# Delta stage of a two-block network: gate softplus in token layout, cumulative sums by a triangular matrix of ones

## The chip, the cores and the metric

The kernel runs on one NeuronCore of a Trainium2 chip. The metric is the device time of one execution in microseconds (us). Its engines are named as the profile names them: PE (TensorE, the matrix products; PEld is its load of the stationary operand), DVE (VectorE), ACT (ScalarE), POOL (GpSimd) and SP (SyncE, which only issues DMAs here). A tensor lies in on-chip memory over 128 partitions; an operation on "16x256" uses 16 partitions and 256 elements in each.

## The reference

The input is one sequence of 256 tokens with 1024 features. Ten stages follow each other, each adding to the residual: twice (hybrid attention, gated FFN with a short convolution), then FFN, short convolution mixer, FFN, FFN, gated DeltaNet mixer ("Delta stage"), FFN. Only the Delta stage is touched. Its projection gives, beside 32 tiles of keys, queries and values, two gates for each of 16 value heads and each token:

```
beta = sigmoid(b)
g    = -exp(a_log) * softplus(a + dt_bias)      # a, b: [token, head]
```

Within each chunk of 128 tokens the stage needs the cumulative sum G of g over the tokens: as a column (token on the partition, one number per head) and as a row broadcast to all partitions (token along the free dimension). exp(G_i - G_j) is the decay between two tokens of a chunk, exp(G_i) the decay of the carried state. The keys' triangular system is solved per head and chunk, and the rest are products.

## The kernel before, in words

All engines run one program in order and are tied by semaphores. The Delta stage's first panel of weights gives the gates (bank 7 of PSUM: b in partitions 0 to 15, a in partitions 32 to 47, tokens along the free dimension). Then slots t = 0 to 46 follow. In slot t (t < 32) PE multiplies tile t of the projection (24 products, L2108 to L2110; every fp32 factor is split into a high and a low part), DVE scales it out of PSUM (delta_read, L1824; PE's tile t waits for the read of tile t-2), ACT starts the convolution (delta_tap, L1164), DVE does its other three taps one slot later (delta_taps, L1831), and ACT applies SiLU and squares (delta_silu, L1184 and L1189). Each slot also splits one panel of weights: ACT makes the high part (L943) and DVE the low part (L1409). Heads go in four sets of four, n = 0 to 3, eight tiles each; delta_step(s, n, o) is what set n does in slot t = 8n + o: rows of G (delta_rows, L2498), masked exponents (delta_exponent, L1898), decays (delta_decay, L1221 and L1229), sums of squared keys (L2508) and key products (delta_kk, L2533), the matrix of the triangular system (delta_amat, L1944). The matrix goes through a relay in HBM (SP: L776, L778) to DVE's solver (L1972, L1973) and back.

Around the change the order is written out by hand in the slot loops of each engine. In slot 1 DVE does the softplus on 16x256 tiles and scans each chunk (delta_gates_softplus, L1855 to L1878). In slot 3 PE transposes the results (delta_turn_gates, L2462), DVE copies them (delta_gates_turned, L1880), ACT takes exp(G) (L1213), and DVE negates it after waiting for ACT (L1889). In slot 4 (ROWS_AT) PE makes the rows of set 0, each by a product of a broadcast unit column with the 16 rows of G. PE's program has the key sums and key products of set 0 right after the transposes in slot 3, and tile 4 behind those. ACT loads a table (ACT_TABLE_LOAD) when the function changes between the groups Exp, Ln, SiLU and Sqrt.

Of the kernel before, what the change touches and what calls it, by code (L numbers as in the profile page):

```python
# [91 lines left out]
def column_map(stages):  # L92

    at, n = {}, 0

    def add(key, count):
        nonlocal n
        at[key] = n
        n += count
    for s, (kind, i) in enumerate(stages):  # L100
        add(("pre", s), KT)
        if kind == HYBRID:
            add(("qk_gain", s), 8)
            add(("cmp_gain", s), 1)
            add(("gate_b", s), 2)
            add(("gla_gain", s), 1)
        if kind == FFN1:
            add(("tap", s), 3 * FT)
            add(("conv_b", s), FT)
        if kind == SHORT:  # L110
            add(("tap", s), 3 * KT)
        if kind == DELTA:
            add(("tap", s), WIDTH * 4 * KH)
            add(("out_norm", s), 1)
            add(("a_log", s), 1)
            add(("dt_bias", s), 1)
    return at, n
# [70 lines left out]
def lay_out(stages, w):  # L188
# [14 lines left out]
    for kind, i in stages:  # L203
# [56 lines left out]
        if kind == DELTA:  # L260
# [15 lines left out]
            late = np.zeros((P, 2), w_in.dtype)  # L276
            late[ROW_A:ROW_A + VH, 0] = w["gdn_a_log_2"][0]
            late[ROW_A:ROW_A + VH, 1] = w["gdn_dt_bias_2"][0]
            cols += [conv_cols, columns(w["gdn_norm_w_2"][0]), late]
# [14 lines left out]
def build(nc, stages, arrays):  # L294
# [14 lines left out]
    with ExitStack() as ctx:  # L309
# [83 lines left out]
        g_cum = carve("g_cum", [ROW_A + VH, S])  # L393
# [4 lines left out]
        a_rate = carve("a_rate", [ROW_A + VH, 1])  # L398
# [534 lines left out]
        def _(act):  # L933
# [267 lines left out]
            def delta_gates(s):  # L1201
# [5 lines left out]
                act.activation(a_rate[a, :], col(("a_log", s))[a, :], ACT.Exp).then_inc(d["gate_act"], 1)  # L1207
# [7 lines left out]
            def delta_decay(s, n):  # L1215
# [8 lines left out]
                act.wait_ge(d["gate_tok"], 3)  # L1224
# [135 lines left out]
            def delta(s):  # L1360
                hi_to(first_panel[s] + 3)
                delta_gates(s)
                for t in range(SLOTS_D):
# [7 lines left out]
                    if t == 3:  # L1371
                        delta_gates_turned(s)
# [22 lines left out]
        def _(dve):  # L1395
# [459 lines left out]
            def delta_gates_softplus(s):  # L1855
                a, b = slice(ROW_A, ROW_A + VH), slice(0, VH)

                dve.wait_ge(d["gate_act"], 1)
                link(dve.tensor_scalar(gates[b, 1, :], gates[b, 1, :], 1.0, None, ALU.add))
                dve.reciprocal(gates[b, 0, :], gates[b, 1, :]).then_inc(d["gates_ready"], 1)  # L1860

                dve.wait_ge(d["gate_act"], 4)
                e, m, ln = gates[a, 2, :], gates[a, 1, :], gates[a, 3, :]
# [7 lines left out]
                link(dve.scalar_tensor_tensor(out=m, in0=gates[a, 0, :], scalar=0.0, in1=ln,  # L1871
                                              op0=ALU.max, op1=ALU.add))
                link(dve.tensor_scalar(e, m, a_rate[a, :], -1.0, ALU.mult, ALU.mult))
# [6 lines left out]
            def delta_gates_turned(s):  # L1880

                dve.wait_ge(d["gate_turned"], 1)
                by_chunk = lambda b, o: bank[b][:, o:o + CHUNKS * VH].rearrange("p (c h) -> p c h", c=CHUNKS)
                dve.tensor_copy(g_tok[:], by_chunk(7, 256)).then_inc(d["gate_tok"], 1)
                dve.tensor_copy(beta_tok[:], by_chunk(6, 0)).then_inc(d["gate_tok"], 1)
                dve.wait_ge(d["gate_tok"], 2)
                dve.tensor_scalar(neg_g[:], g_tok[:], -1.0, None, ALU.mult).then_inc(d["gate_tok"], 1)
                dve.wait_ge(d["tok_exp"], 1)
                link(dve.tensor_scalar(neg_eg[:], neg_eg[:], -1.0, None, ALU.mult))  # L1889
# [215 lines left out]
        def _(pe):  # L2105
# [356 lines left out]
            def delta_turn_gates(s):  # L2462
                pe.wait_ge(d["gates_ready"], 3)
                for c in range(CHUNKS):
                    cs = slice(c * P, (c + 1) * P)
                    o = 256 + VH * c

                    pe.transpose(bank[6][:, VH * c:VH * (c + 1)], gates[0:VH, 0, cs], ident[0:VH, 0:VH])
                    last = pe.transpose(bank[7][:, o:o + VH], g_cum[ROW_A:ROW_A + VH, cs],
                                        ident[ROW_A:ROW_A + VH, ROW_A:ROW_A + VH])  # L2470
                last.then_inc(d["gate_turned"], 1)
# [15 lines left out]
            def delta_rows(s, n):  # L2487
# [243 lines left out]
            def delta(s):  # L2731
                delta_gates(s)
                for t in range(SLOTS_D):
# [37 lines left out]
```

## Time and profile before

| | us |
|---|---|
| median of 3 runs | 2166.47 |
| lowest, highest | 2163.2, 2168.67 |
| the profiled execution | 2163.57 |
| its span in the trace | 2161.8 |
| PE busy in it | 2066.7 (96%) |
| DVE busy | 1447.0 (67%) |
| ACT busy | 1111.4 (51%) |

The span is what the trace covers from the first to the last record; the execution's own time is 1.8 us more. PE's busy share counts a product from its start to its modelled end. The mean granted clock of PE is 0.982 of full speed (2.4 GHz); where it is 0.50 the clock is 1.2 GHz. The Delta stage starts at about 1612 us and ends at about 1885 us of the span.

### The profile page before, as it was taken

The numbers are of one execution on the slowest core, as the hardware profiler recorded it, in microseconds if no ns is written. First come the engines' busy times: TensorE is split into PE (matmuls) and PEld (weight loads), VectorE is DVE, ScalarE is ACT, GpSimd is POOL, SyncE is SP. The second block draws the span as 40 slices with busy tenths as digits, with TensorE's granted clock in tenths as the row PEclk, the third lists the DMA queues.
The fourth block names the chain that finished last, engine by engine and source line by source line (L and its number), as shares of the span: only waits on it lengthen the run. The fifth ranks groups of instructions, "written<-read, shape, count | busy, mean of one in ns | idle before, by whom it ended". The sixth has DMA issues, their size and how long they took to land.

```text
span 2161.8 us, 41596 instructions
## 1 busy us (share of the span) xinstructions
PE 2066.7 (96%) x15668; PEld 1928.9 (89%) x15668; DVE 1447.0 (67%) x2490; ACT 1111.4 (51%) x1802; POOL 49.6 (2%) x63
## 2 busy tenths in 40 slices
PE   7998999999999999999999999999997898999998
PEld 7897889989988899999999999999986898989997
DVE  4567777774677777775567765575668886467555
ACT  4564455554654555554454544454456665546443
POOL 1001000000020000000000000000000000000000
PEclk9999999999999999999999999999998998999999
DMA  8533465553423555555556455555543433335552
GB/s 252 170 118 108 148 208 191 186 171 120 137 98 117 178 192 187 191 179 193 183 159 212 153 194 194 170 187 183 185 168 108 145 112 99 118 132 175 191 184 97
DMA packets 118585, 350.93 MB, mean 162 GB/s; under 512 B 23504, under 2 KB 36120, under 8 KB 117952
## 3 DMA queue, kind: packets, MB, share of 16 engines
q1 hardware_dynamic: 115248, 336.27, 47.2%
q0 software_dynamic: 3216, 12.97, 2.2%
q8 instruction: 85, 1.39, 0.3%
q14 instruction: 36, 0.29, 0.0%
HBM read 341.85 MB, written 7.34 MB: 162 GB/s over the span
## 4 chain that ended last, share of the span: by engine, by line
PE 76%; DVE 12%; ACT 6%; issue 3%; DMA 3%; POOL 0%; SPq 0%; DVEq 0%; ACTq 0%; POOLq 0%
PE bank L2108 23%; PE bank L2110 22%; PE bank L2109 22%; DVE wlo L1409 4%; ACT whi L943 3%; PE bank L2567 2%; DMA raw<-panels 1%; PE bank L2276 1%; DVE arena L1448 1%; DMA relay<-arena 1%; DVE arena L1972 1%; DVE arena L1973 1%; DVE arena L1612 1%; DMA arena<-relay 0%; PE bank L2142 0%
## 5 line engine op out<-in xcount | busy, mean ns | idle before, releaser
L2108 PE MATMUL bank<-xhi,whi 128*128 128x256 f32 x3496 | 1004.4, 287 | 24.6 <-DVE arena L1612 10.1
L2109 PE MATMUL bank<-xlo,whi 128*128 128x256 f32 x3496 | 989.5, 283 | 0.0
L2110 PE MATMUL bank<-xhi,wlo 128*128 128x256 f32 x3496 | 989.0, 283 | 0.0
L1409 DVE TENSOR_TENSOR wlo<-raw,whi 128x1024 fp32r<-128x1024 f32 x623 | 742.4, 1232 | 204.9 <-ACT whi L943 203.9
L2108 PEld LDWEIGHTS bank<-xhi,whi 128*128 128x128 f32 x3496 | 666.2, 191 | 46.3 <-DVE arena L1612 12.5
L2109 PEld LDWEIGHTS bank<-xlo,whi 128*128 128x128 f32 x3496 | 666.2, 191 | 5.4
L2110 PEld LDWEIGHTS bank<-xhi,wlo 128*128 128x128 f32 x3496 | 665.7, 190 | 0.0
L943 ACT ACTIVATE whi<-raw 128x1024 fp32r<-128x1024 f32 x623 | 623.5, 1046 | 49.4 <-DVE arena L1609 19.0
L2108 PE MATMUL bank<-whi,hhi 128*128 128x512 f32 x688 | 274.4, 399 | 2.7 <-DVE hlo L1561 1.2
L2110 PE MATMUL bank<-whi,hlo 128*128 128x512 f32 x688 | 272.8, 397 | 0.0
L2109 PE MATMUL bank<-wlo,hhi 128*128 128x512 f32 x688 | 272.5, 396 | 0.0
L1014 ACT ACTIVATE hhi<-h 128x256 fp32r<-128x256 f32 x172 | 71.9, 418 | 273.6 <-PE bank L2110 151.2
L1561 DVE TENSOR_TENSOR hlo<-h,hhi 128x256 fp32r<-128x256 f32 x156 | 66.4, 426 | 182.3 <-ACT hhi L1014 182.3
L996 ACT ACTIVATE act_out<-first 128x256 f32<-128x256 f32 x92 | 38.4, 418 | 242.0 <-DVE first L1539 235.5
L2110 PEld LDWEIGHTS bank<-whi,hlo 128*128 128x128 f32 x688 | 129.9, 189 | 30.8
L2108 PEld LDWEIGHTS bank<-whi,hhi 128*128 128x128 f32 x688 | 129.9, 189 | 27.9 <-issue 4.6
L2109 PEld LDWEIGHTS bank<-wlo,hhi 128*128 128x128 f32 x688 | 130.4, 190 | 24.6
L1539 DVE TENSOR_TENSOR first<-bank,rstd 128x256 f32<-128x256 f32 x132 | 55.8, 423 | 57.7 <-PE bank L2110 57.4
L1559 DVE TENSOR_TENSOR h<-act_out,second 128x256 f32<-128x256 f32 x136 | 57.9, 426 | 42.1 <-ACT act_out L1005 21.6
L1001 ACT ACTIVATE conv<-first,cols 128x256 f32<-128x256 f32 x44 | 26.5, 602 | 93.1 <-DVE first L1539 93.1
L1061 ACT ACTIVATE arena<-arena 128x256 f32<-128x256 f32 x48 | 20.0, 417 | 102.1 <-DVE arena L1612 102.1
L1540 DVE TENSOR_TENSOR second<-bank,rstd 128x256 f32<-128x256 f32 x132 | 54.9, 416 | 0.0
(361 smaller groups left out, 1708.5 us busy)
## 6 DMA issues: line engine op xcount, KB each, us to landing
raw<-panels SPq DMA_DIRECT2D x623, 512.0 KB, 4.3
arena<-w_in POOLq DMA_DIRECT2D x2, 2048.0 KB, 10.7
arena<-relay SPq DMA_DIRECT2D x8, 512.0 KB, 4.2
arena<-gains_in POOLq DMA_DIRECT2D x6, 512.0 KB, 4.1
relay<-arena POOLq DMA_DIRECT2D x4, 512.0 KB, 7.8
relay<-arena SPq DMA_DIRECT2D x4, 512.0 KB, 5.0
bias_table<-arena POOLq DMA_DIRECT2D x1, 1536.0 KB, 35.1
x<-x_in SPq DMA_DIRECT2D x1, 1024.0 KB, 4.8
```

The costliest lines, as they stand in the source:

```text
L943: act.activation(whi[slot][:], raw[slot][:], ACT.Copy).then_inc(hi_done, 1)
L996: act.activation(act_out[:, sl, :], first[:, sl, 2:], ACT.Silu).then_inc(act_done, 1)
L1014: act.activation(hhi[:, sl, :], h[:, sl, :], ACT.Copy).then_inc(hhi_done, 1)
L1409: dve.tensor_tensor(wlo[slot][:], raw[slot][:], whi[slot][:].bitcast(F32), ALU.subtract) \
L1539: dve.tensor_tensor(first[:, sl, 2:], pair[:, 0:S], rstd[:], ALU.mult).then_inc(gate_scaled, 1)
L1540: dve.tensor_tensor(second[:, sl, :], pair[:, S:], rstd[:], ALU.mult).then_inc(pair_read, 1)
L1559: dve.tensor_tensor(h[:, sl, :], gated, second[:, sl, :], ALU.mult).then_inc(h_done, 1)
L1561: dve.tensor_tensor(hlo[:, sl, :], h[:, sl, :], hhi[:, sl, :].bitcast(F32), ALU.subtract) \
L2108: pe.matmul(dst, w_hi, a_hi, start=start, stop=False, skip_group_check=True)
L2109: pe.matmul(dst, w_hi, a_lo, start=False, stop=False, skip_group_check=True)
L2110: return pe.matmul(dst, w_lo, a_hi, start=False, stop=stop, skip_group_check=True)
L2567: last = pe.matmul(dst[:, m * P:(m + 1) * P], lhs(m), rhs(m), start=True, stop=True)
```

## The change

- The softplus moves from 16x256 tiles (16 partitions, 256 tokens each) to a layout with the token on the partition: 128x32 (two chunks by 16 heads).
- For that, PE turns the raw gates (the exponentials of b and a, the logarithm, and a itself: eight transposes) in slot 2, and DVE's softplus stands in slot 2 instead of slot 1, with the copy out of PSUM and a comparison that makes `until`, the 128x128 matrix of ones on and above the diagonal.
- The two scans go. Slot 3 has instead two products of `until` with the per-token gates.
- The rows of G are made by products of a broadcast gate column (128 partitions) with `until`, one for each head and chunk: eight products of 128 columns for each set of heads, where there were four of 256.
- exp(G) on ACT moves from slot 3 to slot 4 (ROWS_AT), and its negation on DVE to slot 6. The factor exp(a_log) is taken on 128x16, for which the constants get 15 more columns.

```diff
@@ ScalarE, gates
-                act.activation(a_rate[a, :], col(("a_log", s))[a, :], ACT.Exp).then_inc(d["gate_act"], 1)
+                at = col_at[("a_log", s)]
+                act.activation(a_rate, cols[:, at:at + VH], ACT.Exp).then_inc(d["gate_act"], 1)
@@ ScalarE, slot loop
-                    if t == 3:
+                    if t == ROWS_AT:
                         delta_gates_turned(s)
@@ VectorE
             def delta_gates_softplus(s):
-                a, b = slice(ROW_A, ROW_A + VH), slice(0, VH)
-
-                dve.wait_ge(d["gate_act"], 1)
-                link(dve.tensor_scalar(gates[b, 1, :], gates[b, 1, :], 1.0, None, ALU.add))
-                dve.reciprocal(gates[b, 0, :], gates[b, 1, :]).then_inc(d["gates_ready"], 1)
-
+
+                dve.tensor_scalar(until, masks[:, 2, :], -1.0, None, ALU.is_ge).then_inc(d["gates_ready"], 1)
+                dve.wait_ge(d["gate_turned"], 1)
                 dve.wait_ge(d["gate_act"], 4)
-                e, m, ln = gates[a, 2, :], gates[a, 1, :], gates[a, 3, :]
+                m, pre, e, ln = (gates_turned[:, v, :, :] for v in range(4))
+                by = lambda v: v.rearrange("p (c h) -> p c h", c=CHUNKS)
+                link(dve.tensor_copy(gates_turned[:, 1:, :, :].rearrange("p v c h -> p (v c h)"),
+                                     bank[7][:, CHUNKS * VH:4 * CHUNKS * VH]))
+                link(dve.tensor_scalar(m, by(bank[6][:, 0:CHUNKS * VH]), 1.0, None, ALU.add))
+                link(dve.reciprocal(beta_tok[:], m))
...
-                for c in range(CHUNKS):
-                    cs = slice(c * P, (c + 1) * P)
-                    dve.tensor_tensor_scan(g_cum[a, cs], ones[a, :], gates[a, 2, cs], 0.0, ALU.mult, ALU.add) \
-                        .then_inc(d["gates_ready"], 1)
...
+            def delta_gates_summed(s):
+
+                dve.wait_ge(d["gate_turned"], 2)
+                sums = bank[7][:, 256:256 + CHUNKS * VH].rearrange("p (c h) -> p c h", c=CHUNKS)
+                dve.tensor_copy(g_tok[:], sums).then_inc(d["gate_tok"], 1)
+                dve.tensor_scalar(neg_g[:], sums, -1.0, None, ALU.mult).then_inc(d["gate_tok"], 1)
+
+            def delta_gates_negated(s):
+
                 dve.wait_ge(d["tok_exp"], 1)
                 link(dve.tensor_scalar(neg_eg[:], neg_eg[:], -1.0, None, ALU.mult))
@@ VectorE, slot loop
-                    if t == 1:
+                    if t == 2:
                         delta_gates_softplus(s)
                     if t == 3:
-                        delta_gates_turned(s)
+                        delta_gates_summed(s)
+                    if t == ROWS_AT + 2:
+                        delta_gates_negated(s)
@@ TensorE
             def delta_turn_gates(s):
-                pe.wait_ge(d["gates_ready"], 3)
+                pe.wait_ge(d["gate_act"], 4)
+                pe.wait_ge(d["gates_scaled"], 2)
+                pe.wait_ge(rstd_ready, s + 1)
+                for v, (row, i) in enumerate(((0, 1), (ROW_A, 0), (ROW_A, 2), (ROW_A, 3))):
+                    rows = slice(row, row + VH)
+                    for c in range(CHUNKS):
+                        o = (CHUNKS * v + c) * VH
+                        last = pe.transpose(bank[7 if v else 6][:, o:o + VH], gates[rows, i, c * P:(c + 1) * P], ident[rows, rows])
+                last.then_inc(d["gate_turned"], 1)
+
+            def delta_sum_gates(s):
+                pe.wait_ge(d["gates_ready"], 2)
                 for c in range(CHUNKS):
...
+                    last = pe.matmul(bank[7][:, o:o + VH], until, a_tok[:, c, :], start=True, stop=True)
                 last.then_inc(d["gate_turned"], 1)
@@ TensorE, delta_rows
-                        r = ROW_A + SET * n + 2 * g + hh
-                        last = pe.matmul(bank[6 + g][:, hh * S:(hh + 1) * S],
-                                         ident[ROW_A:ROW_A + VH, r:r + 1].to_broadcast([VH, P]),
-                                         g_cum[ROW_A:ROW_A + VH, :], start=True, stop=True)
+                        head = SET * n + 2 * g + hh
+                        for c in range(CHUNKS):
+                            o = hh * S + c * P
+                            last = pe.matmul(bank[6 + g][:, o:o + P], a_tok[:, c, head:head + 1].to_broadcast([P, P]),
+                                             until, start=True, stop=True)
@@ TensorE, slot loop
+                    if t == 2:
+                        delta_turn_gates(s)
                     if t == 3:
-                        delta_turn_gates(s)
+                        delta_sum_gates(s)
```

The order of instructions on three engines follows. Line numbers of the changed kernel are 2 to 13 higher: the read L1824 is L1827 there, the taps L1831 are L1834, the low split L1409 is L1412, on ACT L943 is L945, L1184 is L1186, on PE L2508 is L2521 and L2533 is L2546.

DVE before, slots 1 and 2: the second read and the taps of tile 0, then the gates, then the third read.

```order
L1824 TENSOR_TENSOR arena<-bank5,rstd 128x256
L1831 SCALAR_TENSOR_TENSOR conv<-arena,cols,conv 128x256 x3
L1859 TENSOR_SCALAR arena<-arena 16x256
L1860 RECIPROCAL arena<-arena 16x256
L1864 TENSOR_SCALAR arena<-arena 16x256
L1865 TENSOR_TENSOR arena<-arena 16x256
L1866 SCALAR_TENSOR_TENSOR arena<-arena 16x256
...
L1877 SCALAR_TENSOR_TENSOR arena<-ones,arena 16x128 x2
L1409 TENSOR_TENSOR wlo5<-raw5,whi5 128x1024
L1824 TENSOR_TENSOR arena<-bank4,rstd 128x256
```

DVE now, the same slots.

```order
L1827 TENSOR_TENSOR arena<-bank5,rstd 128x256
L1834 SCALAR_TENSOR_TENSOR conv<-arena,cols,conv 128x256 x3
L1412 TENSOR_TENSOR wlo5<-raw5,whi5 128x1024
L1827 TENSOR_TENSOR arena<-bank4,rstd 128x256
L1834 SCALAR_TENSOR_TENSOR conv<-arena,cols,conv 128x256 x3
L1860 TENSOR_SCALAR arena<-masks 128x128
L1865 COPY arena<-bank7 128x96
L1867 TENSOR_SCALAR arena<-bank6 128x32
L1868 RECIPROCAL arena<-arena 128x32
L1870 TENSOR_SCALAR arena<-arena 128x32
...
L1878 SCALAR_TENSOR_TENSOR arena<-arena 128x32
```

The split of a panel, the read of tile 2 and the taps of tile 1 now stand ahead of the gates. Eleven operations on 16 partitions have become twelve on 128.

PE before, slot 3, behind tile 3: transposes, key sums, key products.

```order
L2468 MATMUL bank6<-masks,arena 128x16
L2469 MATMUL bank7<-masks,arena 128x16
L2468 MATMUL bank6<-masks,arena 128x16
L2469 MATMUL bank7<-masks,arena 128x16
L2508 MATMUL bank3<-ones,sq 128x1 x4
L2533 MATMUL bank2<-arena 128x128 x4
```

PE now: the eight transposes behind tile 2, and behind tile 3 the two sums ahead of key sums and products.

```order
L2115 MATMUL bank4<-xhi,wlo3 128x256
L2475 MATMUL bank6<-masks,arena 128x16 x2
L2475 MATMUL bank7<-masks,arena 128x16 x6
L2113 MATMUL bank5<-xhi,whi4 128x256
...
L2482 MATMUL bank7<-arena 128x16 x2
L2521 MATMUL bank3<-ones,sq 128x1 x4
L2546 MATMUL bank2<-arena 128x128 x4
```

What tile 4 waits behind in PE's order is the same but for the sums; the transposes stand one tile earlier.

ACT before, end of slot 3 and slot 4, from the SiLU of tile 2 to the exponentials of set 0.

```order
L1184 ACTIVATE arena<-conv 128x256
L1189 ACTIVATE sq<-arena 128x256
L1213 ACT_TABLE_LOAD
L1213 ACTIVATE arena<-arena 128x32
L1164 ACTIVATE conv<-arena,cols 128x256
L943 ACTIVATE whi2<-raw2 128x1024
L1184 ACT_TABLE_LOAD
L1184 ACTIVATE arena<-conv 128x256
L1189 ACTIVATE sq<-arena 128x256
L1221 ACT_TABLE_LOAD
L1221 ACTIVATE arena<-bank6 128x256
```

ACT now.

```order
L1186 ACTIVATE arena<-conv 128x256
L1191 ACTIVATE sq<-arena 128x256
L1166 ACTIVATE conv<-arena,cols 128x256
L945 ACTIVATE whi2<-raw2 128x1024
L1186 ACTIVATE arena<-conv 128x256
L1191 ACTIVATE sq<-arena 128x256
L1216 ACT_TABLE_LOAD
L1216 ACTIVATE arena<-arena 128x32
L1224 ACTIVATE arena<-bank6 128x256
```

Two of three table loads are gone, and the small exponential of G stands directly ahead of those of the rows.

## Rows read from the trace of the kernel before

**Rows 1.** The page: span, and the chain that ended last by engine.

```profile
span 2161.8 us, 41596 instructions
...
PE 76%; DVE 12%; ACT 6%; issue 3%; DMA 3%; POOL 0%; SPq 0%; DVEq 0%; ACTq 0%; POOLq 0%
```

**Rows 2.** Busy time by window: length, engines' busy us (instructions), clock, DMA share, GB/s.

```profile
1612.00:1640.90 28.90, 19.83 (x128) 18.98 (x126) 20.55 (x40) 15.35 (x24) 3.24 (x4) 0.76 0.50 167
```

**Rows 3.** Timeline of DVE, slot 1: start, duration, engine, line, [idle before].

```profile
1621.63 1.52 DVE L1831 SCALAR_TENSOR_TENSOR conv<-arena,cols,conv 128x256 f32<-128x256 f32 x3
1623.06 0.28 DVE L1859 TENSOR_SCALAR arena<-arena 16x256 f32<-16x256 f32 x1
1623.37 1.74 DVE L1860 RECIPROCAL arena<-arena 16x256 f32<-16x256 f32 x1
...
1628.54 0.73 DVE L1877 TENSOR_TENSOR_SCAN arena<-ones,arena 16x128 f32<-16x128 f32 x2
```

**Rows 4.** Timeline of PE, slots 3 and 4.

```profile
1621.77 0.39 PE L2108 MATMUL bank<-xhi,whi 128*128 128x256 f32 x1 [2.23 <-DVE arena L1824]
...
1626.13 0.28 PE L2110 MATMUL bank<-xhi,wlo 128*128 128x256 f32 x1
1629.32 0.29 PE L2468 MATMUL bank<-masks,arena 16*128 16x16 f32 x1 [2.92 <-DVE arena L1877]
...
1633.24 1.87 PE L2508 MATMUL bank<-ones,sq 128*128 128x1 f32 x8 [3.53 <-ACT sq L1189]
1634.97 2.05 PE L2533 MATMUL bank<-arena 128*128 128x128 f32 x8
1636.68 0.56 PE L2108 MATMUL bank<-xhi,whi 128*128 128x256 f32 x1
...
1640.84 1.99 PE L2498 MATMUL bank<-arena,masks 16*128 16x256 f32 x8
```

**Rows 5.** Timeline of ACT, slots 1 to 4.

```profile
1624.97 0.42 ACT L1189 ACTIVATE sq<-arena 128x256 f32<-128x256 f32 x1
...
1632.78 0.42 ACT L1189 ACTIVATE sq<-arena 128x256 f32<-128x256 f32 x1
...
1642.88 1.28 ACT L1184 ACT_TABLE_LOAD   x1
...
1645.06 1.28 ACT L1221 ACT_TABLE_LOAD   x1
```

**Rows 6.** Timeline of DVE, slots 4 and 5.

```profile
1640.95 0.42 DVE L1824 TENSOR_TENSOR arena<-bank,rstd 128x256 f32<-128x256 f32 x1 [1.66 <-PE bank L2110]
...
1648.28 2.30 DVE L1944 SCALAR_TENSOR_TENSOR arena<-bank,arena 128x128 f32<-128x128 f32 x8 [0.52 <-ACT arena L1229]
...
1651.16 1.22 DVE L1409 TENSOR_TENSOR wlo<-raw,whi 128x1024 fp32r<-128x1024 f32 x1
```

**Rows 7.** Groups by shape, DVE, whole span: count, busy us, mean ns, idle before.

```profile
L1795 DVE TENSOR_SCALAR second<-second,row_inv 128x128 f32<-128x128 f32 x12 | 3.4, 287 | 0.4
...
L1655 DVE RECIPROCAL qk_inv<-qk_ms 128x32 f32<-128x32 f32 x2 | 0.7, 354 | 0.1
...
L1884 DVE COPY arena<-bank 128x32 f32<-128x32 f32 x1 | 0.2, 183 | 0.0
L1887 DVE TENSOR_SCALAR arena<-arena 128x32 f32<-128x32 f32 x1 | 0.2, 181 | 0.0
```

**Rows 8.** The chain in order of time, two pieces on PE (start, us, what).

```profile
1724.07 1.92 PE bank L2498 x8
...
1729.88 1.78 PE bank L2567 x16
```

**Rows 9.** Busy time by window where PE's clock was lowered, columns as in Rows 2.

```profile
1629.00:1639.20 10.20, 6.35 (x32) 6.24 (x33) 7.81 (x16) 6.05 (x10) 0.00 (x0) 0.50 0.30 103
...
1888.50:1898.60 10.10, 8.73 (x28) 7.45 (x29) 3.01 (x9) 2.41 (x5) 0.00 (x0) 0.50 0.00 1
```

**Rows 10.** One line's instructions on PE: duration of one, min/median/max ns.

```profile
L2567 PE MATMUL bank<-arena x256: 272/275/580, 1678.6 to 1879.6; 128*128 128x128 f32 x128
```

More of the change, by code:

```diff
@@ L114, in column_map @@
             add(("out_norm", s), 1)
-            add(("a_log", s), 1)
+            add(("a_log", s), VH)
             add(("dt_bias", s), 1)
@@ L275, in lay_out @@
             conv_cols = w["gdn_conv_w_2"][0].reshape(WIDTH, 4 * KH, P)[:, order].reshape(-1, P).T
[L276 to L279, printed above, removed]
+            rates = np.repeat(w["gdn_a_log_2"][0][None, :], P, 0)
+            late = np.zeros((P, 1), w_in.dtype)
+            late[ROW_A:ROW_A + VH, 0] = w["gdn_dt_bias_2"][0]
+            cols += [conv_cols, columns(w["gdn_norm_w_2"][0]), rates, late]
         if kind == FFN1:
@@ L392, in build @@
         o_all = carve("o_all", [P, 2 * SET, S])
-        g_cum = carve("g_cum", [ROW_A + VH, S])
+        until = carve("until", [P, P])
+        gates_turned = carve("gates_turned", [P, 4, CHUNKS, VH])
+        a_tok = carve("a_tok", [P, CHUNKS, VH])
         blk_a = carve("blk_a", [P, BLK * BLK])
@@ L397, in build @@
         blk_tmp = carve("blk_tmp", [P, BLK * BLK // 4])
-        a_rate = carve("a_rate", [ROW_A + VH, 1])
+        a_rate = carve("a_rate", [P, VH])
         g_tok = carve("g_tok", [P, CHUNKS, VH])
@@ L1223, in delta_decay @@
                                    ACT.Exp).then_inc(d["eg"], 1)
-                act.wait_ge(d["gate_tok"], 3)
+                act.wait_ge(d["gate_tok"], 2)
                 for g in range(KSET):
@@ L1869, in delta_gates_softplus @@
                 link(dve.tensor_tensor(ln, ln, m, ALU.add))
-                link(dve.scalar_tensor_tensor(out=m, in0=gates[a, 0, :], scalar=0.0, in1=ln,
-                                              op0=ALU.max, op1=ALU.add))
-                link(dve.tensor_scalar(e, m, a_rate[a, :], -1.0, ALU.mult, ALU.mult))
-                for c in range(CHUNKS):
-                    cs = slice(c * P, (c + 1) * P)
-                    dve.tensor_tensor_scan(g_cum[a, cs], ones[a, :], gates[a, 2, cs], 0.0, ALU.mult, ALU.add) \
-                        .then_inc(d["gates_ready"], 1)
[L1880 to L1887, printed above, removed]
+                link(dve.scalar_tensor_tensor(out=m, in0=pre, scalar=0.0, in1=ln, op0=ALU.max, op1=ALU.add))
+                dve.scalar_tensor_tensor(out=a_tok, in0=m, scalar=-1.0,
+                                         in1=a_rate.rearrange("p (o h) -> p o h", o=1).to_broadcast([P, CHUNKS, VH]),
+                                         op0=ALU.mult, op1=ALU.mult).then_inc(d["gates_ready"], 1)
+            def delta_gates_summed(s):
[4 more added lines that the diff above has]
+            def delta_gates_negated(s):
                 dve.wait_ge(d["tok_exp"], 1)
@@ L2462, in delta_turn_gates @@
             def delta_turn_gates(s):
-                pe.wait_ge(d["gates_ready"], 3)
+                pe.wait_ge(d["gate_act"], 4)
[9 more added lines that the diff above has]
+                pe.wait_ge(d["gates_ready"], 2)
                 for c in range(CHUNKS):
-                    cs = slice(c * P, (c + 1) * P)
                     o = 256 + VH * c
-                    pe.transpose(bank[6][:, VH * c:VH * (c + 1)], gates[0:VH, 0, cs], ident[0:VH, 0:VH])
-                    last = pe.transpose(bank[7][:, o:o + VH], g_cum[ROW_A:ROW_A + VH, cs],
-                                        ident[ROW_A:ROW_A + VH, ROW_A:ROW_A + VH])
+                    last = pe.matmul(bank[7][:, o:o + VH], until, a_tok[:, c, :], start=True, stop=True)
                 last.then_inc(d["gate_turned"], 1)
```

## The prediction

> **What bounds the kernel now.** I read the chain of waits first. 76% of the span is PE [rows 1], and the reader should see that almost everywhere the kernel is a row of products that nothing outside PE shortens. So a change in VectorE work pays only where PE waits. Next I read busy time by window: in the 28.90 us from the start of the Delta stage to the end of its tile 4, PE is busy 19.83 us, at a mean clock of 0.76 [rows 2]. The head of this stage is a place where PE waits, for 9 us.
>
> The timelines say for what. Tile 3 starts at 1621.77, when DVE has read tile 1, and its last product, which starts at 1626.13, ends at 1626.41; then PE waits 2.92 us for DVE's scan, transposes at 1629.32, and waits 3.53 us for ACT's square of the second key tile (1632.78 + 0.42 = 1633.20) [rows 4, 5]. That square is late because DVE does the taps of tile 1 behind the gates: the gates hold DVE from 1623.06 to 1628.54 + 0.73 = 1629.27, 6.2 us, of which the reciprocal on 16x256 is 1.74 [rows 3]. Behind the square come key sums and key products (1633.24 to 1636.68, 3.44 us) and tile 4 (1636.68 to 1640.84, 4.16 us) [rows 4]. DVE, which has nothing left, reads tile 4 at 1640.95 after 1.66 us of idleness [rows 6]. From there set 0 goes through ACT's exponentials, DVE's matrix (L1944), the relay and the solver; everything later in the kernel hangs on this chain.
>
> **The change part by part.**
>
> *VectorE, slots 1 and 2.* The taps of tile 0 end at about 1623.1 [rows 3]. Now the split of a panel, the read of tile 2 and the taps of tile 1 follow at once: 1.22 + 0.42 + 1.52 [rows 3, 6] = 3.2, so they end at 1626.3. The gates follow: `until`, one 128x128 operation, 0.29 [rows 7]; a copy of 128x96 out of PSUM, between 0.18 (128x32) and 0.29 (128x128), taken as 0.25 [rows 7]; the addition, 0.18; the reciprocal of 128x32, 0.35, where the one of 16x256 took 1.74 [rows 3, 7]; eight operations of 128x32 at 0.18 = 1.44 [rows 7]. Sum 2.5, and with gaps of 0.03 behind each of twelve linked operations (as from 1623.06 + 0.28 to 1623.37 [rows 3]) 2.9. They end at 1629.2, practically when they end now. The bounds for this block are 2.5 (no gaps) and 3.5 (every small operation as long as the 128x128 one: 12 x 0.29). So the gates are not earlier; what is earlier is the square of tile 1. Its ACT work (tap, split, SiLU, square) took from the end of the third read to 1633.20. Counted from the square of tile 0, which ends at 1625.39 [rows 5], it needs the same four operations: I put its end at 1627.8, an estimate, with 1.5 us to spare. This wait, which ends last now, is then covered.
>
> *TensorE, slots 2 and 3.* The eight transposes fall into the 2.23 us that PE waits ahead of tile 3 [rows 4]. Four of the kind are seen to start within about 0.15 us and take 0.29 each, so eight need less than a microsecond: hidden, and they cost their length only if that cover were gone. What they wait for (the gates of ACT) is done before tile 2 ends, since ACT's program has them ahead of the tap of tile 0. The two sums wait for the gates at 1629.2 and take some 0.3 (bounds 0.1 and 0.6, from the same 0.29 records). Then key sums and products start at 1629.4 rather than 1633.24: 3.8 us earlier. Late next is the gates' last operation, no longer a square. Queued behind the sums are the key sums, the key products and tile 4, so all of them move: tile 4 runs from 1632.9 and ends at 1637.0 rather than 1640.84. I keep the durations, 3.44 and 4.16, because the clock was 0.50 over the whole of 1629.0 to 1639.2 [rows 9], and PE has again been mostly idle ahead.
>
> *VectorE and ScalarE, slots 3 and 4.* DVE's two small operations of slot 3 replace four, and its wait for ACT's exp(G) goes to slot 6; DVE idles before tile 4 anyway, so 0. On ACT the table load of 1.28 ahead of tile 3's SiLU goes [rows 5], because SiLU stays loaded; the load ahead of the exponentials stays, and behind it comes the small exponential (about 0.2). This makes the decays 1.0 us earlier after tile 4. DVE waits for them only 0.52 us before L1944 [rows 6]; its own work (taps of tile 4) ends there, so 0.5 is what comes through, and the split at 1651.16, behind which SP sends the relay, is earlier by that. Bounds: 0.2 and 1.0. Only one set has this order, once.
>
> *Rows of G.* Per set, eight products of 128 columns on 128 rows, so 16 records, for four products of 256 columns on 16 rows, 8 records in 1.92 us on the chain. The nearest row is 16 records of fp32 128x128 with 128 columns in 1.78 us [rows 8]. So -0.14 a set if they overlap alike; if they did not overlap at all, 16 x 0.275 = 4.4, +2.5 a set [rows 10]. Each has a broadcast column as the stationary operand, as the products of the unit column have now, so I take the overlapped price, 0 for four sets, and keep -0.6 and +9.9 as ends.
>
> Here the Trainium skill speaks against the change: "TensorE: Matmul & The Clock Gate", section "LDWEIGHTS (loading the stationary operand)", says that a load costs its columns, 128/1.2 = 107 ns, however few rows it has, so narrow stationary operands were no dearer, and the change doubles the loads. Paid in full, 8 more loads in 4 sets would be an estimated 3.4 us, and the sum would be a gain of 0.9 instead of 4.3. But 16 records in 1.78 us [rows 8] already hold a load each, so the trace does not charge them.
>
> *The rest.* The 15 more columns of constants are loaded at the start with the others: 0.
>
> **Sum.** 3.8 + 0.5 = 4.3 us earlier at the relay of set 0. After that no engine has anything that did not move with it: SP's loads are released by DVE's splits, the solver by the relay, and the last stage is products. So the shift should arrive at the end. Against the profiled execution that is 2163.57 - 4.3 = 2159.3. That one lies 2.9 below the median of the three runs; against the median it is 2166.47 - 4.3 = 2162.2, my forecast. The spread of the three runs is 5.5 us, as large as the gain. What can move it is the clock: stretches at 0.50 of 10.20 and 10.10 us with PE busy 6.35 and 8.73 [rows 9] cost half of that busy time, 3.2 and 4.4 us. A shift of the chain by 4 us can lengthen or shorten such a stretch: +-3 us, an estimate.
>
> **The rivals.**
>
> *The clock comes back earlier.* With less idleness in the head, PE may be at 2.4 GHz for key products and tile 4. Against it: it still idles about 3 us after tile 3. For it: one wait where there were two, and transposes in a third. Key sums and products at half their price are 1.7 rather than 3.44, tile 4, half of whose 4.16 us was slow, loses about 1.2: 2.9 more in all, 2159.3. Shorter slow stretches later could take it to 2156.5.
>
> *The gain is lost on the way.* A slow stretch grows at the end of the stage, where PE is nearly full, or the square of tile 1 is not ready after all, because the panel that ACT splits ahead of it lands late. Half of one such stretch, 3 us, or the 3.8 of the square, leaves 2166. The DMA share of 0.50 in the head [rows 2] makes a late panel unlikely.
>
> *Slower: the row products do not overlap.* One mechanism, on PE ahead of tile 5 of every set, where L2498 stands on the chain at 1.92 [rows 8]. It decides from 3.0 us a set (4.3/4 = 1.08 more), that is 0.19 us a record. At 0.275 a record [rows 10] it costs +9.9, total +5.6: 2172.1; if each is also preceded by its own load it is beyond 2173. For it: stationary and moving operands are now full 128 rows and there are twice as many. Against it: all other fp32 products of this shape overlap to 0.11 us.
>
> **How the numbers follow.** Forecast, 2162.2, own range 2159 to 2166: 0.55. Clock earlier, 2159.3: 0.22. Gain lost, 2166: 0.17. Rows not overlapped, 2172.1: 0.06. This kernel can be told from no change at about 0.3%, 6.5 us: faster means below 2160.0, slower above 2173.0. Faster gets most of the clock's case and a little of the forecast's, 0.19 + 0.07 = 0.26; slower 0.04; the rest, 0.70, is within 0.3%. The range, 2156.5 to 2168.5, holds the first three cases and leaves about 0.1 on either side.
>
> **What would show it.** In the changed profile PE's wait ahead of the key sums is gone and the one ahead of the sums of gates is about 2.8 us, ended by DVE's last gate operation; twelve gate operations in 2.5 to 3.5 us; the read of tile 4 at 1637 (the stage starting alike); one table load of ACT between it and the exponentials; L1944 6.8 us after that read instead of 7.3; rows of G at 1.8 to 2.0 us per set. Wrong would be: a wait on a square ahead of the key sums, row products above 3 us, or a solver of set 0 that starts at 1661 as now.

## The result and the profile after

| | before | changed |
|---|---|---|
| median on the same chip, us | 2164.84 (4 runs) | 2152.44 (4 runs, 2151.41 to 2153.32) |
| ratio to before, 95% interval | 1 | 0.994 [0.9923, 0.9958] |
| profiled execution | 2163.57 | 2152.31 |
| its span | 2161.8 | 2150.5 |
| PE busy | 2066.7 | 2054.4 |

The changed kernel is 12.4 us faster by the medians and 11.3 by the spans. Forecast were 4.3. The forecast, 2162.2, and the whole range down to 2156.5 lie above the result. The 0.6% is beyond the 0.3% that can be told from no change.

The head of the Delta stage comes first, since it is where the prediction looked. DVE of the changed kernel, slots 0 to 5 of the stage (answers to [rows 3, 6]):

```profile
1615.63 0.42 DVE L1827 TENSOR_TENSOR arena<-bank,rstd 128x256 f32<-128x256 f32 x1
...
1619.05 1.52 DVE L1834 SCALAR_TENSOR_TENSOR conv<-arena,cols,conv 128x256 f32<-128x256 f32 x3
1620.48 0.22 DVE L1860 TENSOR_SCALAR arena<-masks 128x128 f32<-128x128 f32 x1
...
1621.13 0.35 DVE L1868 RECIPROCAL arena<-arena 128x32 f32<-128x32 f32 x1
...
1623.09 0.19 DVE L1878 SCALAR_TENSOR_TENSOR arena<-arena 128x32 f32<-128x32 f32 x1
...
1631.70 0.42 DVE L1827 TENSOR_TENSOR arena<-bank,rstd 128x256 f32<-128x256 f32 x1 [4.19 <-PE bank L2115]
...
1638.39 2.15 DVE L1947 SCALAR_TENSOR_TENSOR arena<-bank,arena 128x128 f32<-128x128 f32 x8
...
1650.87 0.17 DVE L1975 TENSOR_TENSOR arena<-arena 64x15 f32<-64x15 f32 x1 [0.62 <-DMA arena<-relay]
```

PE of the changed kernel, slots 2 to 4 (answers to [rows 4]):

```profile
1613.62 0.55 PE L2475 MATMUL bank<-masks,arena 16*128 16x16 f32 x8
...
1616.10 0.56 PE L2113 MATMUL bank<-xhi,whi 128*128 128x256 f32 x1 [1.94 <-DVE arena L1827]
...
1623.34 1.03 PE L2482 MATMUL bank<-arena 128*128 128x16 f32 x4 [2.61 <-DVE arena L1878]
1624.21 1.85 PE L2521 MATMUL bank<-ones,sq 128*128 128x1 f32 x8
1625.92 2.05 PE L2546 MATMUL bank<-arena 128*128 128x128 f32 x8
1627.62 0.56 PE L2113 MATMUL bank<-xhi,whi 128*128 128x256 f32 x1
...
1631.50 1.95 PE L2512 MATMUL bank<-arena 128*128 128x128 f32 x16
```

The reader should see one wait of 2.61 us ahead of the sums of gates (L2482), ended by DVE's last gate operation, and no wait on a square ahead of the key sums (L2521) where [rows 4] have 3.53. The transposes (0.55) run ahead of a wait of PE that is there anyway. ACT of the changed kernel has one table load between the last square and the exponentials (answers to [rows 5]):

```profile
1621.40 0.42 ACT L1191 ACTIVATE sq<-arena 128x256 f32<-128x256 f32 x1
...
1633.59 0.42 ACT L1186 ACTIVATE arena<-conv 128x256 f32<-128x256 f32 x1
1634.04 0.42 ACT L1191 ACTIVATE sq<-arena 128x256 f32<-128x256 f32 x1
1634.48 1.28 ACT L1216 ACT_TABLE_LOAD   x1
1635.77 0.23 ACT L1216 ACTIVATE arena<-arena 128x32 f32<-128x32 f32 x1
```

From DVE's read of tile 1 (1621.29 before, 1615.63 after) to its read of tile 4 (1640.95 [rows 6]; 1631.70) the kernel before takes 19.66 us and the changed one 16.07: 3.6 less. That is close to the forecast. But the read of tile 1 itself comes 5.7 us earlier, and in both kernels the gates stand behind that read; of what the diff changes only the eight transposes of PE (0.55 us) and ACT's exponential of a_log, now on 128x16, can stand ahead of it. The gain began long before this stage. At the other end, the last stage, an FFN that the diff does not touch, is shorter too. The same two DVE operations, one early in that stage and the kernel's last, first before:

```profile
1914.29 0.43 DVE L1559 TENSOR_TENSOR h<-arena,second 128x256 f32<-128x256 f32 x1
...
2154.76 2.74 DVE L1463 SCALAR_TENSOR_TENSOR x<-arena,post_rstd,x 128x512 f32<-128x512 f32 x4
```

and in the changed kernel:

```profile
1905.03 0.43 DVE L1562 TENSOR_TENSOR h<-arena,second 128x256 f32<-128x256 f32 x1
...
2143.48 2.74 DVE L1466 SCALAR_TENSOR_TENSOR x<-arena,post_rstd,x 128x512 f32<-128x512 f32 x4
```

The lead is 5.7 us at the read of tile 1, 10.3 at the first operation of the solver (1661.14 before, 1650.87 after), 9.3 early in the last stage and 11.3 at the end. So 5.7 + 2.0 us come from stages without a changed instruction, and 3.6 from between. Where in the earlier stages the lead arises shows DVE's split of the same two panels, first before:

```profile
935.63 1.23 DVE L1409 TENSOR_TENSOR wlo<-raw,whi 128x1024 fp32r<-128x1024 f32 x1 [0.78 <-ACT whi L943]
...
1596.87 1.23 DVE L1409 TENSOR_TENSOR wlo<-raw,whi 128x1024 fp32r<-128x1024 f32 x1 [0.52 <-ACT whi L943]
```

and in the changed kernel:

```profile
936.20 1.23 DVE L1412 TENSOR_TENSOR wlo<-raw,whi 128x1024 fp32r<-128x1024 f32 x1 [0.78 <-ACT whi L945]
...
1591.04 1.23 DVE L1412 TENSOR_TENSOR wlo<-raw,whi 128x1024 fp32r<-128x1024 f32 x1 [0.52 <-ACT whi L945]
```

At 936 us the changed kernel is still 0.6 us behind. Between these two splits (called the long section below) it takes 654.8 us and the kernel before 661.2: 6.4 us less, the whole lead. The section is one of almost pure products. Busy time by window in the kernel before, columns as in Rows 2:

```profile
860.00:1240.00 380.00, 378.21 (x2716) 355.12 (x2715) 262.68 (x397) 192.21 (x282) 1.06 (x2) 1.00 0.54 180
1240.00:1600.00 360.00, 359.14 (x2531) 335.65 (x2531) 222.27 (x316) 167.60 (x238) 0.53 (x1) 1.00 0.56 184
```

and in the changed kernel:

```profile
860.00:1240.00 380.00, 377.12 (x2729) 353.91 (x2728) 264.54 (x401) 193.37 (x284) 1.06 (x2) 1.00 0.54 182
1240.00:1600.00 360.00, 358.70 (x2559) 335.76 (x2559) 225.56 (x324) 171.73 (x248) 0.53 (x1) 1.00 0.56 185
```

PE is full in both and its granted clock 1.00 in both, yet in the same 740 us it does 5288 products instead of 5247. These 41, at 740/5247 = 0.141 us each, are 5.8 us. A product itself is quicker. Timeline of PE, a product and the 21st behind it, before:

```profile
1010.48 0.28 PE L2108 MATMUL bank<-xhi,whi 128*128 128x256 f32 x1
...
1012.97 0.28 PE L2108 MATMUL bank<-xhi,whi 128*128 128x256 f32 x1
```

and in the changed kernel:

```profile
1010.31 0.28 PE L2113 MATMUL bank<-xhi,whi 128*128 128x256 f32 x1
...
1012.77 0.28 PE L2113 MATMUL bank<-xhi,whi 128*128 128x256 f32 x1
```

That is 2.49/21 = 118.6 ns from start to start against 2.46/21 = 117.1. Over all products of 256 columns between 800 and 1000 us that start within 130 ns of the one before, the mean is 118.4 and 116.8 ns (called the pace below). The kernel has 3 x 3496 = 10488 such products, so 1.6 ns each would be 16.8 us if PE always ran at that pace; where it waits or its clock is lowered, the pace is not collected.

### The profile page after: what moved, and what is told of

Same layout as the page of the kernel before. It is cut to its first block and busy times, and to the rows that moved or that the text cites. A ratio compares the mean times of both kernels' runs of the same rounds, so it can differ in the third digit from the quotient of the medians.

```text
span 2150.5 us, 41675 instructions
## 1 busy us (share of the span) xinstructions
PE 2054.4 (96%) x15708; PEld 1920.4 (89%) x15708; DVE 1441.9 (67%) x2489; ACT 1108.5 (52%) x1800; POOL 49.6 (2%) x63
## 3 DMA queue, kind: packets, MB, share of 16 engines
HBM read 341.86 MB, written 7.34 MB: 162 GB/s over the span
## 5 line engine op out<-in xcount | busy, mean ns | idle before, releaser
L1412 DVE TENSOR_TENSOR wlo<-raw,whi 128x1024 fp32r<-128x1024 f32 x623 | 742.1, 1231 | 202.4 <-ACT whi L945 201.1
L945 ACT ACTIVATE whi<-raw 128x1024 fp32r<-128x1024 f32 x623 | 623.5, 1046 | 50.7 <-DVE arena L1612 20.7
```

The costliest lines, as they stand in the source:

```text
L945: act.activation(whi[slot][:], raw[slot][:], ACT.Copy).then_inc(hi_done, 1)
L1412: dve.tensor_tensor(wlo[slot][:], raw[slot][:], whi[slot][:].bitcast(F32), ALU.subtract) \
```

## The experiments

What the diff changes for those stages is one thing: the constants `cols` grow from 435 to 450 columns. With its padding this tensor takes 1824 instead of 1760 bytes of each partition, and everything declared behind it (`ones`, `x`, the moving operands `xhi`, `xlo`, `hhi`, `hlo`, the arena) lies 64 bytes further. The split weights `whi` and `wlo`, declared ahead of it, stay. **Theory A**: the address of the moving operand relative to the weights sets the pace, and the new table only happens to move it. **Rival B**: the edit of the Delta stage does it, or something in its code that also works elsewhere. **Rival C**: the tensors behind `xhi` and `xlo`, in which most other engines work, are what matters.

Placements below are bytes in a partition. `xhi` starts at 96 modulo 128 before and at 32 after; the weights at 0 in both. The three groups of runs are from three chips, each with its own runs of before: medians 2163.89 (e1 to e4), 2165.96 (e5 to e8) and 2164.64 (e9 to e12). Ratios with their intervals are to these runs; they are not quotients of the medians and differ from them by up to 0.0009. A difference between runs of two groups carries the difference of the chips with it, up to 2 us.

### e1: only the shift

```diff
         cols = sb("cols", [P, n_cols])
+        gap = sb("gap", [P, 16])
```

> The kernel before, with an unused tensor of 64 B per partition behind the constants, so that every later tensor of on-chip memory starts where it starts in the changed kernel. No instruction differs. Theory A (the 5.9 us gained before the Delta stage and 2.0 us in the last stage come from the addresses): about 8 us faster, 2157, products of 256 columns 116.8 ns apart instead of 118.4. Rival B (they come from where the constants lie in HBM, from the code or from the runs): no change, 2165.

Measured: 2156.98, ratio 0.9973 [0.9962, 0.9985], pace 116.9 ns. The kernel before, with 64 unused bytes in it, is 6.9 us faster, and its long section takes 654.9 us, as in the changed kernel. Window of e1:

```profile
1240.00:1600.00 360.00, 358.69 (x2558) 335.52 (x2556) 226.22 (x325) 171.87 (x250) 0.53 (x1) 1.00 0.55 184
```

2558 products, as the changed kernel's 2559, where before has 2531. No instruction of the Delta stage differs here, so rival B cannot explain this.

### e2: the change with the old addresses

```diff
         cols = sb("cols", [P, n_cols])          # in the changed kernel
+        gap = sb("gap", [P, 112])
```

This puts `xhi` at 96 modulo 128 again, and at the same place modulo 512 as before.

> The changed kernel with 448 B unused behind the constants: later tensors lie 512 B above their place in the kernel before, so at the same place in every 512 B. Theory A: about 8 us slower than the changed kernel, 2160.5, and products 118.4 ns apart again; then the rest, about 4 us against before, is the edit of the Delta stage, as forecast (4.3). Rival B: stays at 2152.4.

Measured: 2161.56, 0.9991 [0.9982, 1.0001], pace 118.35. Window of e2:

```profile
1240.00:1600.00 360.00, 359.15 (x2531) 335.57 (x2530) 222.54 (x316) 167.25 (x236) 0.53 (x1) 1.00 0.55 184
```

The long section takes 661.2 us again. At the old placement the change gives 2.3 us against before, with an interval of the ratio that holds 1. At the new placement it gives 2156.98 - 2152.44 = 4.5 against e1, or 5.5 when each is taken from its own chip's before (12.4 and 6.9). By the whole time the edit of the Delta stage is thus worth a few microseconds, not told more exactly; 4.3 was the forecast.

### e3 and e4: other shifts of the kernel before

`gap` of 8 columns (e3, 32 bytes, `xhi` at 0 modulo 128) and of 24 (e4, 96 bytes, `xhi` at 64).

> The kernel before with 32 B unused: the moving operands xhi and xlo then start at a multiple of 128 B. Theory A: another time than before (2165) and than e1, product spacing different; if what counts is a start at a multiple of 64 or 128 B, it is the fastest, 2155 or below. Rival B: 2165.

> The kernel before with 96 B unused: xhi at 64 in 128 B, hhi at 32 in 64 B. If theory A holds with a multiple of 64 B, like e3; if what counts is the hhi tensors, at 64 B multiples in both given kernels, slower than before. Rival B: 2165.

Measured: e3 2177.23, 1.0061 [1.0039, 1.0083], pace 119.7. e4 2163.8, 0.9994 [0.9984, 1.0004], pace 117.8. The timeline of e3, again 21 products apart:

```profile
1010.25 0.28 PE L2109 MATMUL bank<-xhi,whi 128*128 128x256 f32 x1
...
1012.77 0.28 PE L2109 MATMUL bank<-xhi,whi 128*128 128x256 f32 x1
```

2.52/21 = 120.0 ns. So 32 unused bytes cost 13 us and 64 gain 7: the same program spreads over 20 us by its addresses alone. The pace does not order all times: e4 has a better pace than before and the same time. Its products of 512 columns (moving operand `whi` or `wlo`, stationary `hhi` or `hlo`) are slower: 234.3 ns apart against 233.0.

The long section shows both kinds at once, without the scatter of whole executions. In every kernel it has 3702 products of 256 columns and 872 of 512 (means taken within the section):

| | `xhi` modulo 128 | long section, us | 256 columns, ns | 512 columns, ns |
|---|---|---|---|---|
| before, e2, e11 | 96 | 661.2 | 118.4 | 233.0 |
| e8 | 96 | 660.3 | 118.3 | 232.0 |
| e12 | 48 | 661.3 | 118.3 | 233.3 |
| e4 | 64 | 660.1 | 117.8 | 234.3 |
| e3 | 0 | 666.8 | 119.7 | 233.9 |
| e10 | 32 | 658.7 | 118.6 | 228.2 |
| changed, e1, e5, e6, e9 | 32 | 654.8 to 654.9 | 116.8 | 231.6 to 231.7 |
| e7 | 32 | 654.9 | 116.7 | 232.7 |

The two paces account for the lengths: e4 has 3702 x 0.6 = 2.2 us less and 872 x 1.3 = 1.1 more, -1.1 where -1.2 is measured; e3 has +5.7 for +5.6, e10 -3.2 for -2.5, the changed kernel -6.9 for -6.4.

### e5: only the order of VectorE

```diff
-                    if t == 1:                  # in e1
+                    if t == 2:
                         delta_gates_softplus(s)
```

The gates keep 16x256 tiles and scans but stand behind the taps of tile 1; the 64 bytes of e1 are in.

> The kernel before at the changed kernel's addresses (e1, 2157.0) with one edit: the softplus in its old layout stands in slot 2 instead of slot 1. Theory A (the new layout makes the gain of the Delta stage, the order alone only moves the wait): the square of the second key tile is early, but the gates end 6.2 us behind the taps of tile 1, at about 1632.5 on the clock of the trace before, so the key sums start 0.4 us earlier than before: 2156.6. Rival B (the order makes the gain): 3 us or more below e1, 2154 or less.

Measured: 2156.07, 0.9963 [0.9951, 0.9974]; the interval overlaps that of e1. DVE's second read and its read of tile 4 in e5:

```profile
1614.88 0.42 DVE L1825 TENSOR_TENSOR arena<-bank,rstd 128x256 f32<-128x256 f32 x1
...
1634.33 0.42 DVE L1825 TENSOR_TENSOR arena<-bank,rstd 128x256 f32<-128x256 f32 x1 [1.45 <-PE bank L2111]
```

19.45 us where before has 19.66 and the change 16.07. The same stretch in e1, e3, e4, e7, e8 and e11, whose head is that of before, takes 19.3 to 20.4, and in e2, e6, e9, e10 and e12, whose head is the changed one, 15.9 to 16.9. So the layout's gain is clear of the scatter and the order alone gives nothing that is. PE of e5:

```profile
1625.99 0.29 PE L2469 MATMUL bank<-masks,arena 16*128 16x16 f32 x1 [6.02 <-DVE arena L1878]
...
1626.32 1.86 PE L2509 MATMUL bank<-ones,sq 128*128 128x1 f32 x8
```

The wait on the square is gone and the one on the gates has grown from 2.92 to 6.02, about the 2.92 + 3.53 of [rows 4]. The head is paid either way; only gates that are shorter *and* behind the taps shorten it. The layout is what makes them fit: 6.2 us of gates become 2.8.

### e6: exp(G) and its negation in slot 3

```diff
-                    if t == ROWS_AT:            # ScalarE, in the changed kernel
+                    if t == 3:
                         delta_gates_turned(s)
-                    if t == ROWS_AT + 2:        # VectorE
+                    if t == 3:
                         delta_gates_negated(s)
```

> The changed kernel (2152.4) with exp(G) on ACT and its negation on DVE both back in slot 3. ACT loads tables once more in slots 3 and 4 and DVE waits in slot 3. Theory A (this part is worth the 0.5 to 1.0 us seen between the read of tile 4 and the start of the solver): 2153.0 to 2153.5. Rival B (it is hidden behind tile 4): 2152.4, and L1947 starts 6.7 us after the read of tile 4 as in the changed kernel.

Measured: 2155.28, 0.9958 [0.9942, 0.9975]: 2.8 above the changed kernel's 2152.44, or 1.7 when each is taken from its own chip's before; the intervals of the two ratios overlap. DVE of e6:

```profile
1627.86 0.18 DVE L1892 TENSOR_SCALAR arena<-arena 128x32 f32<-128x32 f32 x1 [2.28 <-ACT arena L1216]
...
1630.89 0.42 DVE L1827 TENSOR_TENSOR arena<-bank,rstd 128x256 f32<-128x256 f32 x1 [1.59 <-PE bank L2115]
...
1638.22 2.30 DVE L1947 SCALAR_TENSOR_TENSOR arena<-bank,arena 128x128 f32<-128x128 f32 x8 [0.56 <-ACT arena L1232]
```

L1947 starts 7.33 us after the read of tile 4 instead of 6.69: this part is worth 0.64, nearly all of it the 0.56 that DVE waits again. It is 7.33 or 7.34 in all nine traces with exp(G) in slot 3, and 6.69 in the changed kernel, e2, e10 and e12. The wait of 2.28 in slot 3 costs nothing: 1.59 of idleness is left behind it, and the read of tile 4 comes 16.07 us behind that of tile 1 as in the changed kernel. The other 2 us of the profiled execution appear after 1680 us, away from the edit, and I did not find their cause.

### e7 and e8: which tensor's address

```diff
+        gap_a = sb("gap_a", [P, 16])            # e7 only
         xhi = sb("xhi", [P, KT, S], F32R)
         xlo = sb("xlo", [P, KT, S], F32R)
+        gap_b = sb("gap_b", [P, 112])           # e7; 16 columns in e8
```

e7 moves `xhi` and `xlo` by 64 bytes and what follows by 512; e8 moves only what follows, by 64.

> The kernel before with 64 B unused ahead of xhi and 448 B behind xlo: only xhi and xlo lie 64 B further in every 512 B, all later tensors keep their place in it. Theory A1 (the place of the moving operand xhi, xlo against the weights decides): products of 256 columns 116.9 ns apart, 6 to 7 us faster than before, 2157 to 2158. Rival A2 (the later tensors, hhi and hlo or the arena, decide): 118.4 ns, 2164.

> The kernel before with 64 B unused behind xlo: xhi and xlo stay, hhi, hlo, the arena and the rest move by 64 B. Theory A1: spacing of the 256-column products 118.4 ns, 2162 to 2164 (the 512-column products with hhi and hlo as stationary operand may win 1 ns each, 2 us). Rival A2: 2157.

Measured: e7 2154.89, 0.9957 [0.994, 0.9974], pace 116.7; e8 2167.3, 1.0003 [0.9992, 1.0014], pace 118.3. Timeline of e7:

```profile
1015.28 0.28 PE L2110 MATMUL bank<-xhi,whi 128*128 128x256 f32 x1
...
1017.73 0.28 PE L2110 MATMUL bank<-xhi,whi 128*128 128x256 f32 x1
```

and of e8:

```profile
1015.31 0.28 PE L2109 MATMUL bank<-xhi,whi 128*128 128x256 f32 x1
...
1017.79 0.28 PE L2109 MATMUL bank<-xhi,whi 128*128 128x256 f32 x1
```

2.45 against 2.48 us for 21 products. Moving the two moving operands brings the whole effect on the products of 256 columns, moving what follows none. What e8 moves does change those of 512 (233.0 to 232.0 ns), 0.9 us of the long section, too little to show in the whole time. Rival C falls for the 256 columns. The 4 us between e7 (11.1 below its chip's before) and e1 (6.9) are not the pace, since their long sections are equal; the intervals of the ratios overlap.

### e9: the rows of G twice

```diff
                             o = hh * S + c * P
-                            last = pe.matmul(bank[6 + g][:, o:o + P], a_tok[:, c, head:head + 1].to_broadcast([P, P]),
-                                             until, start=True, stop=True)
+                            for again in range(2):
+                                last = pe.matmul(bank[6 + g][:, o:o + P],
+                                                 a_tok[:, c, head:head + 1].to_broadcast([P, P]),
+                                                 until, start=True, stop=True)
```

> The changed kernel with each row product of every set made twice (the second overwrites the first with the same numbers). Theory (row products overlap and stand on the path of each set): 1.7 to 1.9 us more in each of four sets, 7 us, 2159.5. Rival (rows of sets 1 to 3 are covered by other work): 2 us or less. If the products did not overlap: 4 us a set, 2168.

Measured: 2159.77, 0.9977 [0.9967, 0.9988], 7.3 above the changed kernel. PE of e9, ahead of tile 5:

```profile
1632.38 3.73 PE L2513 MATMUL bank<-arena 128*128 128x128 f32 x32
```

32 records in 3.73 us, against 16 in 1.95: 1.8 us a set, four sets, 7.1. So the rows stand on the path in full, and their price is the overlapped one that the forecast took.

### e10: 128 bytes further

```diff
         cols = sb("cols", [P, n_cols])          # in the changed kernel
+        gap = sb("gap", [P, 32])
```

`xhi` keeps its place modulo 128 and moves from 416 to 32 modulo 512, with the weights at 128.

> The changed kernel with 128 B unused behind the constants. If the place counts within 128 B, the spacing of the 256-column products stays at 116.8 ns and the time at 2152.4; if it counts within 512 B, both change.

Measured: 2156.04, 0.9962 [0.9951, 0.9973], 3.6 above the changed kernel; pace 118.7, but the products of 512 columns go from 231.7 to 228.2 ns. Timeline of e10, 2.50 us for 21 products:

```profile
1010.04 0.28 PE L2114 MATMUL bank<-xhi,whi 128*128 128x256 f32 x1
...
1012.54 0.28 PE L2114 MATMUL bank<-xhi,whi 128*128 128x256 f32 x1
```

The place modulo 128 alone does not decide: the pattern repeats over more than 128 bytes, and it is another for the two kinds of product.

### e11: the weights moved as well

```diff
+        gap = sb("gap", [P, 16])                # in the kernel before
         whi = [sb(f"whi{i}", [P, KT * P], F32R) for i in range(RING)]
```

`xhi` lies where the changed kernel has it, but as far from the weights as before.

> The kernel before with 64 B unused ahead of the split weights: whi, wlo and all behind them lie 64 B further, so xhi lies where it lies in the changed kernel (e1, 2157.0, and e7, 2154.9), but its distance from the weights is that of the kernel before. If the place of xhi itself decides: 116.9 ns, 2157. If the distance between moving and stationary operand decides: 118.4 ns, 2164.

Measured: 2168.03, 1.0014 [1.0002, 1.0026], pace 118.4. It is 3.4 above before, but not by the pace: the profiled execution falls behind that of before in its first 250 us, and its long section takes 661.2 us as before. Timeline of e11:

```profile
1015.45 0.28 PE L2109 MATMUL bank<-xhi,whi 128*128 128x256 f32 x1
...
1017.93 0.28 PE L2109 MATMUL bank<-xhi,whi 128*128 128x256 f32 x1
```

2.48 us, as in e8. The place of `xhi` alone does not decide (e11), nor that of the weights alone (e1); the distance between the two fits every run. The products of 512 columns say the same: `hhi` lies in e11 where the changed kernel has it, but as far from the weights as before, and they start 233.0 ns apart, as before. Two things stay open. e11 also moved `cols`, and the 512 columns are not set by the distance alone: `hhi` is equally far from the weights in e4 and e12, with 234.3 and 233.3 ns.

### e12: 16 bytes further

```diff
-        xhi = sb("xhi", [P, KT, S], F32R)       # in the changed kernel
-        xlo = sb("xlo", [P, KT, S], F32R)
+        x_parts = sb("x_parts", [P, 2 * KT * S + 8], F32R)
+        xhi, xlo = (x_parts[:, 4 + j * KT * S:4 + (j + 1) * KT * S].rearrange("p (k n) -> p k n", k=KT)
+                    for j in range(2))
```

> The changed kernel with xhi and xlo in one tensor and 16 B further, at 48 in 128 B, which none of the runs had; later tensors move by 32 B. The four places tried so far gave 119.7 (0), 116.9 (32), 117.7 (64) and 118.4 ns (96). If 32 is a peak of a smooth curve, 117.2 and 2154; if half-lines of 32 B are what counts, slower, 2160; a better place than 32 would be below 116.5 ns and 2150.

Measured: 2164.39, 0.9998 [0.9987, 1.0009], pace 118.3: 12 us above the changed kernel by 16 bytes (the tensors behind lie 32 further, a step that no other run takes by itself). Of these 12, 6.4 are the long section, 661.3 us. The profiled execution, at 2158.97 the fastest of the ten, still has the gain of the Delta stage (16.9 us from the read of tile 1 to that of tile 4); why the median is 5.4 above it is not known. None of the twelve beats the changed kernel.

## Why the prediction was wrong

The mechanism in the Delta stage was right. The step that failed stands under *The rest*: "The 15 more columns of constants are loaded at the start with the others: 0." No run prices loading them, but the term is not 0: they shift the addresses of `xhi` and `xlo` against the weights, and that measured 6.9 us in e1 (0.9973) and 11 in e7 (0.9957). By place in the traces: 6.4 us in the long section, in both, and 2.0 in the last stage. The forecast had looked for an effect of the change only where its instructions stand, so the range held nothing of the kind.

Term by term:

- *Head, forecast 3.8.* 3.6. One wait of 2.61 (2.8 forecast) where there were two. From the end of tile 3 to the key sums it is 1624.21 - 1620.73 = 3.48 for 1633.24 - 1626.41 = 6.83, so 3.35; the forecast had the sums of gates too short. The last 0.2 come from tile 4. The square of tile 1 ends at 1621.40 + 0.42 = 1621.82, 1.5 us ahead of the sums, as forecast. e5 shows that the reordering alone is worth 0.2 here.
- *Gates, 2.9 (2.5 to 3.5).* From 1620.48 to 1623.09 + 0.19 = 1623.28: 2.8, for twelve operations; before there were twelve as well, not eleven.
- *Sums of gates, 0.3 (0.1 to 0.6).* 1624.21 - 1623.34 = 0.87, outside the bounds. They are two fp32 products, four records, of 128x128 weights; the 0.29 records that I took have 16 partitions.
- *Transposes, 0.* 0.55 us, and behind them PE still waits 1.94 for the read of tile 1. They cost nothing.
- *exp(G) to slot 4, 0.5 (0.2 to 1.0).* 0.64 by e6's place of L1947. e6 as a whole is 1.7 to 2.8 us slower, of which the rest is unexplained.
- *Rows of G, 0 (-0.6 to +9.9).* 1.95 us for 16 records against 1.99 for 8 [rows 4]. e9 shows that they are on the path. Not overlapping, the rival on the slower side, did not happen.
- *Sum.* 4.3 forecast; 4.6 from the read of tile 1 to the solver of set 0 (10.3 - 5.7). Over the traces this stretch takes 39.5 to 41.2 us with the old head (before, e1, e3, e4, e7, e8, e11) and 35.1 to 36.3 with the new (the changed kernel, e2, e10, e12), so the gain at the solver is shown. That all of it reaches the end is not: at equal addresses the medians give 2.3 (e2), and against e1 4.5 or 5.5.

The parts add up to the spans: 5.7 before the Delta stage, 4.6 in its head, -1.0 from the solver to the last stage (10.3 to 9.3, cause not found) and 2.0 in the last stage are 11.3. The rival *the clock comes back earlier* had the direction and one part of the place, but key sums and products took 3.41 us (forecast 3.44) and tile 4 3.88 (1627.62 to 1631.50; forecast 4.16). The granted clock is back at 1.00 2.2 us after tile 4 starts, at 1629.81, where before it took 2.6. So the clock gave 0.3 us where the rival had 2.9. That its 2159.3 lies nearer to the result is chance.

## What to carry to other kernels

When a kernel is full of products back to back, an edit that changes the size of any tensor on chip can change the pace of every product whose operands it moves against each other. Compare the start-to-start time of the same product in both traces, far from the edit, before crediting the edit; then repeat the comparison with padding that restores the old addresses. And a forecast of a change that adds or grows a tensor needs a term with bounds for it, here from 13 us lost (e3) to 7 gained (e1).

## What the runs showed of the hardware

- fp32r products of 256 columns with 128x128 weights, clock 1.00, start 116.7 to 119.7 ns apart, by the distance between the moving operand and the weights in on-chip memory. Distances modulo 128 of 96 (before, e2, e8, e11) give 118.3 to 118.4; 32 (after, e1, e7) 116.7 to 116.9; 64 (e4) 117.8; 0 (e3) 119.7; 48 (e12) 118.3. e10, at 32 but elsewhere in 512, gives 118.7.
- The difference between the placements does not come from other engines or DMAs. Over whole traces, where no record of DVE, ACT or POOL and no DMA packet lies within 0.1 us of a product, the mean is still 118.5 ns in before, e2, e8 and e11 (269 products) and 117.1 in the changed kernel, e1, e5, e6, e7 and e9 (402).
- That points to PE's own reads, of the moving operand and of the next weights. That these two get in each other's way is argued, not shown. The Trainium skill says the opposite, in "TensorE: Matmul & The Clock Gate", section "Step-by-step: what each phase is for": two independent read ports, so that loading the next weights doesn't take bandwidth from the running product. e11 against the changed kernel differs from that: with `xhi` at one place and only the weights and `cols` elsewhere, the pace went from 116.8 to 118.4.
- Left open: how the reads collide, over how many bytes the pattern repeats, and whether a placement better than the changed kernel's exists for both kinds of product (e10's 228.2 ns for 512 columns says one may).
- Records of fp32 products with a broadcast column as weights overlap to 0.12 us each (16 in 1.95, 32 in 3.73), though each holds its own load of 128 columns.
